# Router logits of an expert-choice encoder layer: products with the tokens stationary against products with the router weights stationary, in four column quarters

## What is computed

```python
h2 = rms_norm(x, norm2_g)
aff = softmax((h2 @ w_router).astype(float32), axis=-1)     # [n, 16]
gates, idx = lax.top_k(aff.T, cap)                          # cap = n / 8
xe = xt[idx]
a = einsum('ecd,edf->ecf', xe, w_gate); u = einsum('ecd,edf->ecf', xe, w_up)
ye = einsum('ecf,efd->ecd', silu(a) * u, w_down) * gates
```

## Time and profile before

| | |
|---|---|
| median of 3 executions | 1525.65 us (1525.55, 1525.65, 1528.02) |
| profiled execution | 1527.59 us, its span 1525.8 us |
| TensorE | busy 98% of the span, mean granted clock 0.993 |
| VectorE, ScalarE, GpSimd | busy 82%, 71%, 11% |
| memory traffic | 448 MB, 294 GB/s on average |

### The profile page before, as it was taken

The page is one execution under the profiler, slowest core; times in us unless marked ns, Lnnn a source line. Parts: engine busy times, 40 slices in busy tenths (PEclk is TensorE's granted clock), DMA queues, the critical chain, the costliest instruction groups (busy, mean ns, idle before and its releaser), DMA issues.

```text
span 1525.8 us, 18627 instructions
## 1 busy us (share of the span) xinstructions
PE 1491.8 (98%) x7265; PEld 1225.0 (80%) x7265; DVE 1247.6 (82%) x1151; ACT 1090.8 (71%) x1231; POOL 169.2 (11%) x123
## 2 busy tenths in 40 slices
PE   7999999999999999999999999999999999999997
PEld 7787877677878888888888888888888888888886
DVE  4358778775688888888989888898988888898985
ACT  7555456875467878787787878777777878778774
POOL 1013131000010201010110101011010101101010
PEclk9999999999989999999999999999999999999999
DMA  6111102202679999999999999999999999999993
GB/s 235 56 55 56 56 26 86 99 1 85 261 263 385 376 387 371 395 377 394 374 387 385 369 395 378 393 376 388 383 376 393 376 394 375 393 376 387 392 379 113
DMA packets 192246, 447.98 MB, mean 294 GB/s; under 512 B 13272, under 2 KB 13600, under 8 KB 192160
## 3 DMA queue, kind: packets, MB, share of 16 engines
q1 hardware_dynamic: 187776, 434.08, 76.5%
q0 software_dynamic: 4224, 12.65, 3.6%
q10 hardware_dynamic: 160, 0.07, 0.0%
HBM read 434.19 MB, written 12.58 MB: 293 GB/s over the span
## 4 chain that ended last, share of the span: by engine, by line
PE 89%; DVE 5%; ACT 3%; issue 1%; DMA 1%; POOLq 0%; POOL 0%; DVEq 0%; ACTq 0%
PE ps L996 23%; PE ps L998 23%; PE ps L997 23%; PE ps L655 4%; PE ps L657 4%; PE ps L656 4%; PE ps L1031 1%; DVE states L1553 1%; PE ps L882 1%; PE ps L914 1%; PE ps L989 1%; PE ps L976 1%; DMA h_sample_rows<-hn 1%; PE ps L898 1%; ACT wih L1092 0%
## 5 line engine op out<-in xcount | busy, mean ns | idle before, releaser
L1922 DVE TENSOR_TENSOR wl<-raw,wh 128x2048 fp32r<-128x2048 f32 x384 | 873.1, 2289 | 126.2 <-ACT wh L1401 124.5
L1401 ACT CAST wh<-raw 128x2048 fp32r<-128x2048 f32 x384 | 731.3, 1913 | 124.7 <-PE ps L998 123.2
L996 PE MATMUL ps<-wh,XTh 128*128 128x512 f32 x1024 | 404.9, 395 | 0.9 <-issue 0.9
L998 PE MATMUL ps<-wl,XTh 128*128 128x512 f32 x1024 | 399.5, 390 | 0.0
L997 PE MATMUL ps<-wh,XTl 128*128 128x512 f32 x1024 | 398.5, 389 | 0.0
L998 PEld LDWEIGHTS ps<-wl,XTh 128*128 128x128 f32 x1024 | 192.2, 188 | 41.0
L996 PEld LDWEIGHTS ps<-wh,XTh 128*128 128x128 f32 x1024 | 192.3, 188 | 38.9 <-issue 1.1
L997 PEld LDWEIGHTS ps<-wh,XTl 128*128 128x128 f32 x1024 | 192.5, 188 | 38.1
L996 PE MATMUL ps<-wh,gTh 128*128 128x512 f32 x512 | 200.9, 392 | 0.0
L998 PE MATMUL ps<-wl,gTh 128*128 128x512 f32 x512 | 199.4, 390 | 0.0
L997 PE MATMUL ps<-wh,gTl 128*128 128x512 f32 x512 | 199.2, 389 | 0.0
(11 more groups left out here) (248 smaller groups left out, 1585.3 us busy)
## 6 DMA issues: line engine op xcount, KB each, us to landing
raw<-in_w_gate SPq DMA_DIRECT2D x128, 1024.0 KB, 12.1
raw<-in_w_up SPq DMA_DIRECT2D x128, 1024.0 KB, 12.1
raw<-in_w_down SPq DMA_DIRECT2D x128, 1024.0 KB, 12.2
slice_raw<-in_w_in SPq DMA_DIRECT2D x5, 2048.0 KB, 8.0
X<-in_x_sample SPq DMA_DIRECT2D x8, 512.0 KB, 6.5
slice_raw<-in_w_out SPq DMA_DIRECT2D x2, 2048.0 KB, 8.5
X<-in_x_prompt SPq DMA_DIRECT2D x4, 512.0 KB, 7.4
slice_raw<-in_w_in SPq DMA_DIRECT2D x4, 512.0 KB, 7.5
```

The lines of the kernel that those rows point to most:

```text
L996: pe.matmul(out, hi, rhs_h, start=first, stop=False)
L998: return pe.matmul(out, hi, rhs_l, start=False, stop=last)
L1401: act.copy(wh[:, n % CONV, :], raw[:, n % RAW, :]).then_inc(s_wh, 1)
L1922: dve.tensor_tensor(wl[:, n % CONV, :], raw[:, n % RAW, :], wh[:, n % CONV, :].bitcast(F32), ALU.subtract).then_inc(s_wl, 1)
```

## The change

- `wr` gets 32 columns for each block of 128 features, the last 16 cleared (a new VectorE instruction in attention step 13).
- `router_parts(v)` replaces the eight products: the block of `wr` (128x32) is stationary and the block of `h2T` (128 tokens) moves. Feature blocks k and k + 4 go to column quarter k % 4 of the array, that is to PSUM partitions 32(k % 4) onward. The result is, for each quarter, a 32x128 sum, transposed against before. It lies in bank 0 or 1 (bank 4 for tile 1).
- `parts_copied(v)` copies that 128x128 block to SBUF: on ScalarE for tiles 2, 3, 4, 5 and 0, on VectorE for tile 1.
- `router_logits(v)` is now one float32 product of two passes: the copied block stationary, a constant 128x16 `adder` moving (four identity blocks on top of each other, made on VectorE from `ident` in attention step 13). It adds the quarters and turns the sum into tokens by experts, in bank 7 as before.
- On TensorE's list, parts and logits are interleaved with `rows_turned`; on tile 0 all the parts come ahead of the second half of tile 1's transposes. `router_logits(5)` stands behind `diff_turned(0)`.
- `h2T` buffers come free with the parts (`s_part`) and no longer with the logits (`s_lg`).
- VectorE gets the copy of tile 1's parts between the casts L1887 and L1888 and `rows_normed(0)`.
- The unread products: 4 before TensorE waits for `s_aff` 2 and 26 after the affinity transposes. They read `MTh` and `MTl` (operands of the output projection) and no longer wait for ScalarE's `s_wh`.

```diff
+PART_BANK = {2: 0, 3: 1, 4: 0, 5: 1, 0: 0, 1: 4}
-        wr = at("wr", 212480, [P, KD, NE])
+        wr = at("wr", 220672, [P, KD, 32])
+        parts = [at(f"parts{j}", 221696 + 512 * j, [P, P]) for j in range(2)]
+        adder = at("adder", 222720, [P, NE])
...
-            def router_logits(v, steps=range(KD)):
-                c, p = logit_column(v), POS[v]
+            def router_parts(v):
+                p = POS[v]
                 if p == 0:
-                    pe.wait_ge(s_wrg, 1)
-                for k in steps:
+                    pe.wait_ge(s_wrg, 3)
+                for k in range(KD):
                     if k % 4 == 0:
                         pe.wait_ge(s_h2d if k else s_h2a, p + 1)
-                    mm = pe.matmul(ps[:, 7, c:c + NE], h2T[p % 2][:, k, :], wr[:, k, :],
-                                   start=(k == 0), stop=(k == KD - 1))
-                    if k == KD - 1:
-                        mm.then_inc(s_lg, 1)
+                    quarter = slice(32 * (k % 4), 32 * (k % 4) + 32)
+                    mm = pe.matmul(ps[quarter, PART_BANK[v], 0:P], wr[:, k, :], h2T[p % 2][:, k, :],
+                                   start=(k < 4), stop=(k >= 4), skip_group_check=True)
+                mm.then_inc(s_part, 1)
+
+            def router_logits(v):
+                c, p = logit_column(v), POS[v]
+                if v == 1:
+                    pe.wait_ge(s_part_d, 1)
+                else:
+                    pe.wait_ge(s_part_a, p + 1)
+                pe.matmul(ps[:, 7, c:c + NE], parts[p % 2][:], adder[:], start=True, stop=True).then_inc(s_lg, 1)
...
             pe.wait_ge(*fill_read(last_in_bank(7)))
+            router_parts(2)
+            rows_turned(4)
             router_logits(2)
-            rows_turned(4)
+            router_parts(3)
+            rows_turned(5)
             router_logits(3)
-            rows_turned(5)
-            router_logits(4)
+            router_parts(4)
             pe.wait_ge(s_pvc, len(ATT))
             gla_half(0, 1, LAST_BANK[0, 1], None)
+            router_logits(4)
+            router_parts(5)
+            diff_turned(0)
             router_logits(5)
-            diff_turned(0)
...
             rows_turned(1, (0,))
-            router_logits(0, range(0, 4))
+            router_parts(0)
             rows_turned(1, (1,))
-            router_logits(0, range(4, KD))
+            router_logits(0)
+            router_parts(1)
             router_logits(1)
...
+            keep_busy(4)
             pe.wait_ge(s_aff, 2)
...
-                    pe.matmul(ps[:, 0, :], wh[:, 0, 0:P], wh[:, 0, 0:512], start=True, stop=True)
-            pe.wait_ge(s_wh, 1)
-            keep_busy(34)
+                    pe.matmul(ps[:, 0, :].rearrange("p (k c) -> p k c", k=4), MTh[:, 0, 0:P], MTl[:, 0, :, :],
+                              start=True, stop=True)
+            keep_busy(26)
...
+            def parts_copied(v):
+                p = POS[v]
+                act.wait_ge(s_part, p + 1)
+                if p >= 2:
+                    act.wait_ge(s_lg, p - 1)
+                act.copy(parts[p % 2][:], ps[:, PART_BANK[v], 0:P]).then_inc(s_part_a, 1)
...
             for v in ORDER[1:4]:
                 h2_copied(v, 0)
+                parts_copied(v - 1)
                 rows_root(v)
+            parts_copied(5)
...
             h2_copied(1, 0)
+            parts_copied(0)
...
+                    dve.memset(wr[:, :, NE:32], 0.0).then_inc(s_wrg, 1)
+                    dve.tensor_tensor(wr[:, :, 0:NE], wr[:, :, 0:NE], gcol[:].unsqueeze(2).broadcast_to([P, KD, NE]),
+                                      ALU.mult).then_inc(s_wrg, 1)
+                    dve.tensor_reduce(adder[:], ident[:].rearrange("p (g e) -> p e g", g=4)[:, 0:NE, :], AX_X, ALU.add)\
...
             dve.tensor_copy(idxr[32:32 + NE, :], topi[32:32 + NE, ::-1]).then_inc(s_cand, 1)
+            dve.wait_ge(s_part, NT)
+            dve.wait_ge(s_lg, NT - 2)
+            dve.tensor_copy(parts[POS[1] % 2][:], ps[:, PART_BANK[1], 0:P]).then_inc(s_part_d, 1)
             rows_normed(0)
```

More of the change, by code:

```diff
@@ L305, in build @@
             ("router_logits", "router_max", "router_exp", "affinity", "affinity_turned", "affinity_copied"))
+        s_part, s_part_a, s_part_d = (sem(n) for n in
+            ("router_parts", "router_parts_from_act", "router_parts_from_dve"))
         s_vals = sem("top_values_listed")
@@ L463, in _ @@
             sp.wait_ge(s_s, 1)
-            sp.dma_start(wr[:], a["w_router"][0].rearrange("(k p) e -> p k e", p=P)).then_inc(s_wr, 16)
+            sp.dma_start(wr[:, :, 0:NE], a["w_router"][0].rearrange("(k p) e -> p k e", p=P)).then_inc(s_wr, 16)
             with nc.allow_non_contiguous_dma(reason="1024 gains, eight a partition"):
@@ L967, in _, with keep_busy @@
             pe.transpose(ps[0:CAP_S, 3, CAP_S:P], idxr, ident[0:CAP_S, 0:CAP_S]).then_inc(s_topT, 1)
+            def keep_busy(n):
+                for _ in range(n):
+                    pe.matmul(ps[:, 0, :].rearrange("p (k c) -> p k c", k=4), MTh[:, 0, 0:P], MTl[:, 0, :, :],
+                              start=True, stop=True)
+            keep_busy(4)
             pe.wait_ge(s_aff, 2)
@@ L972, in _ @@
             mm.then_inc(s_afT, 1)
-            def keep_busy(n):
-                for _ in range(n):
-                    pe.matmul(ps[:, 0, :], wh[:, 0, 0:P], wh[:, 0, 0:512], start=True, stop=True)
-            pe.wait_ge(s_wh, 1)
-            keep_busy(34)
+            keep_busy(26)
             pe.wait_ge(s_tables, 1)
@@ L1366, in h2_copied @@
                 if p >= 2:
-                    act.wait_ge(s_lg, p - 1)
+                    act.wait_ge(s_part, p - 1)
                 act.copy(h2T[p % 2][:, 4 * f:4 * f + 4, :], ps[:, 2 + f, :].rearrange("p (k c) -> p k c", k=4))\
                     .then_inc(s_h2d if f else s_h2a, 1)
+            def parts_copied(v):
[4 more added lines that the diff above has]
+                act.copy(parts[p % 2][:], ps[:, PART_BANK[v], 0:P]).then_inc(s_part_a, 1)
             def affinity_exp(part, n):
@@ L1763, in beside @@
                     dve.wait_ge(s_wr, 32)
-                    dve.tensor_tensor(wr[:], wr[:], gcol[:].unsqueeze(2).broadcast_to([P, KD, NE]), ALU.mult)\
+                    dve.memset(wr[:, :, NE:32], 0.0).then_inc(s_wrg, 1)
+                    dve.tensor_tensor(wr[:, :, 0:NE], wr[:, :, 0:NE], gcol[:].unsqueeze(2).broadcast_to([P, KD, NE]),
+                                      ALU.mult).then_inc(s_wrg, 1)
+                    dve.tensor_reduce(adder[:], ident[:].rearrange("p (g e) -> p e g", g=4)[:, 0:NE, :], AX_X, ALU.add)\
                         .then_inc(s_wrg, 1)
@@ L1821, in h2_copied @@
                 if p >= 2:
-                    dve.wait_ge(s_lg, p - 1)
+                    dve.wait_ge(s_part, p - 1)
                 dve.tensor_copy(h2T[p % 2][:, 4:8, :], ps[:, 3, :].rearrange("p (k c) -> p k c", k=4)).then_inc(s_h2d, 1)
```

## The result

The changed kernel takes 1530.81 us (median of 19 executions, 1529.08 to 1534.62), the kernel before 1526.03 (19 executions, 1525.22 to 1530.71). The ratio is 1.0029, 95% interval [1.0022, 1.0036]: slower, by 4.4 us of 1526 by the ratio and 4.8 by the two medians. The prediction said 1525.2 in a range up to 1528.8. The profiled execution took 1533.9 us, its span 1532.1 against 1525.8.

A forecast was written before the change was run, and what follows sets the result against it. TensorE was taken to bound the kernel, its expert stage starting when the stage before allows. Attention 0, sample tiles 0, prompt chain 0 and unread products -0.45 us took the median from 1525.65 to 1525.2, range 1523.8 to 1528.8.

The forecast's parts named there:

- The bound: TensorE holds 89% of the chain; the expert stage, 440 to 1500 us, runs at its pace.
- the three points: Waits within 380 to 436 us: sample softmax behind a store, prompt softmax behind last logits, turned rows behind unread products.
- the small terms: Small costs, such as 0.2 us a tile for logits, 0.1 a mode switch, about 0.3 for VectorE's copy.
- 0 (sample tiles): Four sample tiles: 1.6 us less TensorE work only lengthens its idle time before the softmax; effect 0.
- Softmax of the samples hangs on a store: Before the sample softmax: VectorE's last sample rows wait for a store to free its buffer, not for a product.
- Parts at 1.02 us a tile: Router on TensorE: 16 quarter-width passes take 1.02 us a tile, bounds 0.5 and 2.18.
- Prompt chain, net 0: Prompt tiles up to the softmax: VectorE's new copy and wait use up its old 0.89 us wait; 0, bounds ±0.6.
- Unread products, -0.45: Before the turned rows: 26 unread products end ahead of the gather's landing, so the gather ends the stage; 0.45 us gained.
- Rivals A and B: Clock lost at the sample softmax wait (chance 0.22) or before the prompt gather (0.12 alone), 2.7 us each: 1527.9.
- Both together: Clock lost both at the sample softmax wait and before the prompt gather: 1530.6 us, chance 0.08.
- C and D: C: column quarters do not overlap, 1527.2, chance 0.05. D: VectorE's prompt chain is shorter, 1524.3, chance 0.10.

The follow-up runs named there:

- before_new_unread: Kernel before with its own router but the change's unread products (4 ahead of the second softmax wait, 26 behind the transposes): 1528.91 us, ratio 1.0021.
- fill_softmax: Changed kernel with 18 unread products added ahead of the wait for the sample softmax: 1527.38 us, ratio 1.0008.
- fill_softmax_8: Changed kernel with 8 unread products added ahead of the wait for the sample softmax: 1528.18 us, ratio 1.0021.
- act_copy: Changed kernel with 18 unread products before the sample softmax, 12 behind the tables wait, and tile 1's parts copied by ScalarE, not VectorE: 1524.77 us, ratio 0.9989.
- act_copy_early_fill: act_copy plus 6 unread products ahead of the scores of attention heads 1 and 3: 1524.17 us, ratio 0.9982.
- old_unread: Changed kernel with the old unread products (none ahead of the second softmax wait, 34 behind the transposes and ScalarE's first high part): 1528.6 us, ratio 1.0017.

## Why the prediction was wrong

The bound, the three points and the arithmetic of the small terms held. The choice among the cases did not.

The step that failed is the price put on TensorE's idle time: nothing, in two places. For the sample tiles the prediction let the wait before the softmax grow from 2.79 to 4.3 us and entered "0 (sample tiles)" in the sum. For the unread products it let them end ahead of the landing of the gather and entered -0.45. The clock was to hold through both; that it might not was left to the rivals. The runs show 2.44 us lost behind the first wait and 2.48 behind the second, and both losses gone when the waits are filled.

- *Softmax of the samples hangs on a store.* Right: 3.19 us from the last sample rows to the transposes in both traces, whatever TensorE did before.
- *Parts at 1.02 us a tile.* Mis-sized: 0.64 us with the last pass's latency, near the lower bound of 0.5. By the starts of the instructions a pass takes 0.136 us at full width, 0.064 in halves and 0.036 in quarters, 3.8 times less than at full width. The Trainium skill (TensorEngine Tiling (Array Packing), Theoretical Speedup) had up to 4x, and the trace agrees. I had written that this "would only lengthen an idle time", which was true; that the idle time costs nothing was not. The size itself mattered little: two traces with the same code up to there had 4.35 and 4.22 us, as forecast, against 5.05 in this one, and lost the clock as well.
- *Prompt chain, net 0.* Within its bounds: 0.45 us gained. VectorE's wait for the parts was 0.24 and its copy 0.29, as priced, but the copy of tile 1 came no later, since the parts ahead of it were so short. The gain is one over thin products at half clock; thin products at full clock are quicker there than parts (4.53 against 4.94 us).
- *Unread products, -0.45.* The gather did end the stage, for -0.39 us. But the prediction had 26 products end at 432.5 if the clock fell as before, 1.5 us ahead of the landing, and at 429.2 if it did not. At full clock the wait was 4.76 us, as computed. Where the clock did fall it was low for 3.4 us and not for 10, with four unread products ahead of the softmax wait, and PE still waited 3.12 to 3.27 us (before_new_unread, fill_softmax, fill_softmax_8). So in every trace with the new counts and nothing behind the tables the wait was over 3 us and cost the clock. Why the low stretch became shorter was not tested.
- *Rivals A and B.* The mechanism and the price were right: 2.7 us each was forecast, 2.44 and 2.48 measured between events of the traces, 3.2 and 2.7 from the two fills. "Both together" stood at 1530.6, and the median is 1530.81; that the two agree so closely is in part luck, since the kernel before stood at 1526.03 in this comparison and not at 1525.65. I gave it 0.08, as if the falls were accidents of 0.2 each. Both idle times were written into the change, and the evidence against the falls was one wait of 2.79 us that had kept the clock, which says nothing for 4.3 and 4.8.
- *C and D.* Quarters do overlap; and D's shorter chain exists, worth 0.45 us beside losses of 5.
- The Trainium skill (TensorE: Matmul & The Clock Gate, HAM oscillation) says that gaps between bursts of matmuls send the clock back to half. Every trace here agrees for gaps from 3.12 us up; it should have had a larger chance.

## What to carry to other kernels

Work taken off TensorE ahead of a wait that something else sets does not vanish, it turns into idle time, and idle time of the engine can have a price of its own: here some 2.5 us for each of two gaps, paid by the next work. Look at what follows each wait, not only at what precedes it. If unread products are used as a bridge, tie them to the events (a few behind the semaphore that starts the last transfer) and not to a count tuned at one clock: 26 were 4.8 us short at full clock and still 3.1 to 3.3 us short where it had fallen under them, 46 in a row were 2.4 us too many. And where a fall can't be avoided, let it come under work that nobody waits for: between the prompt router and the unread products it only slowed unread products, in act_copy and act_copy_early_fill, two of the three fastest kernels here.

## What the runs showed of the hardware

- Idle TensorE and the clock, at the sample softmax and before the gather, one trace each: it fell, in the gap or within a microsecond behind it, with gaps of 3.12, 3.21, 3.27, 4.22, 4.35, 4.76 and 5.05 us, and stayed at full with 2.13, 2.35, 2.79 and 2.83.
- Between the prompt router and the transposes of its affinities shorter gaps did not decide it. With parts, the clock fell at about 420 us in five of eight traces, around gaps of 1.09, 1.10, 1.61, 1.62 and 2.74 us (act_copy, act_copy_early_fill, fill_softmax_8, fill_softmax, old_unread), and stayed at full in three with 1.61 and 1.62 us. In the kernel before it fell at 419 us under thin products with PE busy all the time. At 135 and 225 us, behind 1.9 us of idle time, it fell in some executions and not in others. What decides there is left open.
- Float32 products of 32 stationary and 128 moving columns in four column quarters: 16 passes in 0.64 us, against 1.09 for 8 at full width. TensorE's weight loads paused 0.17 us ahead of the first tile's parts and 0.20 us behind the third's, much as at the change from halves; ahead of the second and third tile's parts, right behind a full-width product, the profile has no pause.
- Executions of one kernel differ: the kernel before ran between 1524.3 and 1531.7 us in one set of 29 executions, with 11 below 1525.8. With the idle times filled, 12 executions lay within 1.9 us.
